# Attention heads: the division by the softmax sum done in the transposing product, and the rotary columns of two heads in one block

## What is computed

```python
def apply_rope2d(x, ang):
    xr = x.reshape(*x.shape[:-1], 2, 2, ROPE_FREQS)      # ROPE_FREQS = 16
    x1, x2 = xr[..., 0, :], xr[..., 1, :]
    out = jnp.stack([x1 * cos - x2 * sin, x2 * cos + x1 * sin], axis=-2)
    return out.reshape(x.shape)
...
q = (rms(q_a, g_qa) @ w_qb).reshape(b, n, N_HEADS, D_NOPE + D_ROPE)   # 16 x (128 + 64)
s = (q_nope @ k_nope + apply_rope2d(q_rope) @ k_rope) * scale
p = softmax(s)          # latents over 768 keys, context over its own 128
o = p @ v
```

## Time and profile before

| | |
|---|---|
| timed runs, median (lowest to highest) | 3592.96 us (3592.6 to 3592.97) |
| profiled execution | 3597.43 us |
| its span, first to last instruction | 3595.5 us |
| mean granted TensorE clock | 0.957 of full |
| TensorE busy / its weight loads | 3330.1 us (93%) / 2603.1 us (72%) |
| VectorE, ScalarE, GpSimd busy | 2101.0 (58%), 1392.9 (39%), 315.6 us (9%) |
| instructions | 40124 |

### The profile page before, as it was taken

How to read it: one execution, slowest core, us unless ns; L and a number is a source line. 1 busy time by engine, 2 the same in 40 slices (tenths; PEclk the granted TensorE clock), 3 DMA queues, 4 the chain that set the end, 5 groups by cost and what they waited for, 6 DMA issues and landing times. The chain is left out here.

```text
span 3595.5 us, 40124 instructions
## 1 busy us (share of the span) xinstructions
PE 3330.1 (93%) x16242; PEld 2603.1 (72%) x16242; DVE 2101.0 (58%) x1746; ACT 1392.9 (39%) x1234; POOL 315.6 (9%) x383
## 2 busy tenths in 40 slices
PE   6889999999997999987999999657999999999994
PEld 4678878888886999976888888554666666666662
DVE  3346555555453766653233232256888888888884
ACT  3121212221121444432121221125777777777773
POOL 0020010100000000000011210000111111111100
PEclk8999999999998999998999999858999999999997
DMA  9465554465552111106253443329999999999995
GB/s 373 176 171 203 178 185 173 164 240 191 189 176 95 38 38 38 40 19 252 102 182 134 157 169 111 121 97 368 363 398 394 381 396 395 379 398 393 382 400 201
DMA packets 140637, 796.34 MB, mean 221 GB/s; under 512 B 18416, under 2 KB 29552, under 8 KB 57360
## 3 DMA queue, kind: packets, MB, share of 16 engines
q1 hardware_dynamic: 104560, 694.46, 50.2%
q0 software_dynamic: 35952, 100.07, 9.3%
HBM read 726.60 MB, written 67.86 MB: 221 GB/s over the span
## 5 line engine op out<-in xcount | busy, mean ns | idle before, releaser
L104 PE MATMUL i_ps<-w_hi,hT_hi 128*128 128x512 f32 (+1 forms) x1440 | 568.8, 395 | 25.2 <-DVE hT_lo L559 12.9
L105 PE MATMUL i_ps<-w_lo,hT_hi 128*128 128x512 f32 (+1 forms) x1440 | 559.7, 389 | 0.0
L106 PE MATMUL i_ps<-w_hi,hT_lo 128*128 128x512 f32 (+1 forms) x1440 | 559.4, 388 | 0.0
L99 DVE TENSOR_TENSOR w_lo<-w_stage,w_hi 128x2048 fp32r<-128x2048 f32 x192 | 439.3, 2289 | 90.7 <-ACT w_hi L94 90.5
L99 DVE TENSOR_TENSOR w_lo<-w_stage_more,w_hi 128x2048 fp32r<-128x2048 f32 x192 | 439.3, 2289 | 52.2 <-ACT w_hi L94 50.3
L94 ACT ACTIVATE w_hi<-w_stage 128x2048 fp32r<-128x2048 f32 x192 | 368.3, 1919 | 163.9 <-PE e_ps L106 163.9
L94 ACT ACTIVATE w_hi<-w_stage_more 128x2048 fp32r<-128x2048 f32 x192 | 369.4, 1924 | 149.3 <-PE e_ps L106 149.3
L104 PE MATMUL e_ps<-w_hi,xgT_hi 128*80 128x512 f32 x1024 | 403.9, 394 | 6.3 <-DVE w_lo L99 5.0
L105 PE MATMUL e_ps<-w_lo,xgT_hi 128*80 128x512 f32 x1024 | 403.8, 394 | 0.0
L106 PE MATMUL e_ps<-w_hi,xgT_lo 128*80 128x512 f32 x1024 | 401.3, 392 | 0.0
L104 PE MATMUL p_ps<-w_hi,xT_hi 128*128 128x512 f32 x960 | 376.5, 392 | 18.2 <-DVE xT_lo L1437 18.2
(11 more groups left out here) (271 smaller groups left out, 4793.9 us busy)
## 6 DMA issues: line engine op xcount, KB each, us to landing
w_stage<-in_w_e SPq DMA_DIRECT2D x192, 1024.0 KB, 8.3
w_stage_more<-in_w_e SPq DMA_DIRECT2D x192, 1024.0 KB, 8.7
w_stage<-in_w_ada SPq DMA_DIRECT2D x96, 1024.0 KB, 6.0
w_raw<-in_w_in SPq DMA_DIRECT2D x64, 1024.0 KB, 4.9
w_stage<-in_w_o_gm SPq DMA_DIRECT2D x16, 1024.0 KB, 7.6
w_stage<-in_w_o_mla SPq DMA_DIRECT2D x16, 1024.0 KB, 5.7
w_stage<-in_w_out SPq DMA_DIRECT2D x16, 1024.0 KB, 5.0
acts<-evacuated POOLq DMA_DIRECT2D x60, 256.0 KB, 4.1
```

The costliest lines, as they stand in the source:

```text
L99: dve.tensor_tensor(dst, src, hi.bitcast(F32), ALU.subtract).then_inc(st.split, 1)
L104: pe.matmul(out, x_hi, w_hi, start=first, stop=False)
L105: pe.matmul(out, x_hi, w_lo, start=False, stop=False)
L106: return pe.matmul(out, x_lo, w_hi, start=False, stop=last)
```

## The change

In the heads, `divide` no longer scales the tile of probabilities: it scales the identity by the reciprocals into a diagonal matrix `diag`, and `turn` is an ordinary float32 matmul of the unscaled tile with that diagonal in place of a transpose through the identity.

The 64 rotary columns of two heads (each as its first and its second halves, instead of interleaved by 16) share one block of 128 rows, without swapped copies. Its product (`proj_rope(j)`) is done in two parts, one of each 320 tokens, in head `j - 2`. `rotate(j)` turns one such part for both heads; the swapped operand is read from the neighbouring 32 partitions. The weights of an even head have the block (1536 columns), those of an odd one don't (1024). `evac_qr` stands behind the work on the turned tile 1 on ScalarE and VectorE. The cosine and sine table is laid out anew (`table` is 128 x 2 x 640 instead of 128 x 640), and so are the rope columns of the key, of the cached keys and of `w_in`; for this the key's context rows are stored in two parts, so that `ctx_out` counts to 48. Left out below are buffers, layouts made on the host, and waits already named.

```diff
             pool.wait_ge(rot, 2)
-            pool.dma_start(O["new_krope"][0, 0], kr[:, 0, 0:D_ROPE]).then_inc(ctx_out, 16)
+            for h in range(2):
+                pool.dma_start(O["new_krope"][0, 0].rearrange("p (a h f) -> h p a f", a=2, h=2)[h],
+                               kr[:, 0, bass.ts(h, D_ROPE // 2)].rearrange("p (a f) -> p a f", a=2)).then_inc(ctx_out, 16)
...
                         if t == 0:
-                            act.wait_ge(ctx_out, 32)
+                            act.wait_ge(ctx_out, 48)
...
                 dve.tensor_tensor(kr_cos[:], raw, table[:, :, 0:D_ROPE], ALU.mult).then_inc(rot_part, 1)
-                for t in range(TT):
-                    for h in range(2):
-                        one_t = lambda ap: ap[:, t, :].rearrange("p (a h f) -> p a h f", a=2, h=2)
-                        dve.tensor_tensor(one_t(kr_sin)[:, :, h, :], one_t(raw)[:, :, 1 - h, :], one_t(table[:, :, D_ROPE:])[:, :, h, :],
-                                          ALU.mult).then_inc(rot_part, 1)
-                dve.wait_ge(rot_part, 1 + 2 * TT)
+                H = D_ROPE // 2
+                for h in range(2):
+                    dve.tensor_tensor(kr_sin[:, :, bass.ts(h, H)], raw[:, :, bass.ts(1 - h, H)], table[:, :, bass.ts(2 + h, H)],
+                                      ALU.mult).then_inc(rot_part, 1)
+                dve.wait_ge(rot_part, 3)
...
                     sp.wait_ge(pv, n - 1)
-                sp.dma_start(raw[:, n % 2, :], W_H[n]).then_inc(raw_in[n % 2], 16)
+                sp.dma_start(raw[:, n % 2, 0:split_width(n) + HW_V], I["w_heads_b" if n % 2 else "w_heads_a"][n // 2]).then_inc(raw_in[n % 2], 16)
...
             load_head(0)
-            sp.dma_start(table[:], I["rope_cols"]).then_inc(tab_in, 16)
+            sp.dma_start(table[:].rearrange("p a n -> p (a n)"), I["rope_cols"]).then_inc(tab_in, 16)
...
                     act.wait_ge(pk, n - 1)
-                act.activation(part_hi[:, b, :], raw[:, b, 0:HW_Q + HW_K], ACT.Copy).then_inc(w_hi, 1)
+                    act.wait_ge(pr, n)
+                act.activation(part_hi[:, b, 0:split_width(n)], raw[:, b, 0:split_width(n)], ACT.Copy).then_inc(w_hi, 1)
...
             def evac_qr(n):
-                act.wait_ge(rot_sum, n + 1)
-                act.activation(qr[n % 2][0:D_ROPE, :], rot[0][:], ACT.Copy).then_inc(e_hi, 1)
+                act.wait_ge(rot_sum, 2 * (n // 2) + 2)
+                act.activation(qr[n % 2][own(n), :], rot[n // 2 % 2][own(n), :], ACT.Copy).then_inc(e_hi, 1)
...
                 exp(a, 1)
+                turn_hi(a, 1)
...
                     evac_qr(a + 1)
-                turn_hi(a, 1)
...
                 dve.wait_ge(w_hi, n + 1)
-                lo(part_lo[:, b, :], raw[:, b, 0:HW_Q + HW_K], part_hi[:, b, :]).then_inc(w_lo, 1)
+                w = slice(0, split_width(n))
+                lo(part_lo[:, b, w], raw[:, b, w], part_hi[:, b, w]).then_inc(w_lo, 1)
...
-            def rotate(n):
-                dve.wait_ge(pr, n + 1)
-                if n:
-                    dve.wait_ge(e_lo, 4 * n - 2)
-                for c, (x, y) in enumerate(((0, D_ROPE), (D_ROPE, P))):
-                    dve.tensor_tensor(rot[c][:].rearrange("p (c n) -> p c n", c=2), pair[1][x:y, :, 0:N_TOK // 2],
-                                      table[x:y, :].rearrange("p (c n) -> p c n", c=2), ALU.mult).then_inc(rot_part, 1)
-                dve.wait_ge(rot_part, 2 * n + 2)
-                dve.tensor_tensor(rot[0][:], rot[0][:], rot[1][:], ALU.add).then_inc(rot_sum, 1)
+            def rotate(j):
+                dve.wait_ge(pr, j + 1)
+                if j:
+                    dve.wait_ge(rot_sum, j)
+                H = D_ROPE // 2
+                toks = bass.ts(j % 2, N_TOK // 2)
+                dst = rot[j // 2 % 2]
+                dve.tensor_tensor(dst[:, toks], pair[1][:, j % 2, 0:N_TOK // 2], table[:, 0, toks], ALU.mult).then_inc(rot_part, 1)
+                for c in range(4):
+                    dve.tensor_tensor(rot_sin[bass.ts(c, H), :], pair[1][bass.ts(c ^ 1, H), j % 2, 0:N_TOK // 2],
+                                      table[bass.ts(c ^ 1, H), 1, toks], ALU.mult).then_inc(rot_part, 1)
+                dve.wait_ge(rot_part, 5 * j + 5)
+                dve.tensor_tensor(dst[:, toks], dst[:, toks], rot_sin[:], ALU.add).then_inc(rot_sum, 1)
...
                 dve.wait_ge(e_hi, 4 * n + 2)
-                lo(qr[n % 2][D_ROPE:P, :], rot[0][:], qr[n % 2][0:D_ROPE, :]).then_inc(e_lo, 1)
+                lo(qr[n % 2][own(n + 1), :], rot[n // 2 % 2][own(n), :], qr[n % 2][own(n), :]).then_inc(e_lo, 1)
...
                 if u == 0:
-                    dve.tensor_scalar(prob_c[:], prob_c[:], red[:, 3, 1:2], None, ALU.mult)
-                dve.tensor_scalar(prob[u % 2][:], prob[u % 2][:], red[:, 3, cols(u)], None, ALU.mult).then_inc(p_ok, 1)
+                    dve.tensor_scalar(diag[2][:], M.ident[:], red[:, 3, 1:2], None, ALU.mult)
+                dve.tensor_scalar(diag[u % 2][:], M.ident[:], red[:, 3, cols(u)], None, ALU.mult).then_inc(p_ok, 1)
...
             rotate(0)
+            rotate(1)
...
                 divide(a, 1)
-                if ahead:
-                    rotate(a + 1)
+                if a + 2 < HEADS:
+                    rotate(a + 2)
                 top(a, 2)
+                turn_lo(a, 1)
...
                     evac_qr(a + 1)
-                turn_lo(a, 1)
...
         def _(pe):
-            def proj_q(n, which):
+            def proj_q(n):
                 b = n % 2
-                if which == 0:
-                    pe.wait_ge(w_lo, n + 1)
-                    if n:
-                        pe.wait_ge(e_lo, 4 * n - 1)
-                elif n:
-                    pe.wait_ge(e_lo, 4 * n)
-                    if n >= 2:
-                        pe.wait_ge(o_ev, n - 1)
-                c0 = P * which
+                pe.wait_ge(w_lo, n + 1)
+                if n:
+                    pe.wait_ge(e_lo, 4 * n - 1)
                 for half in range(2):
-                    for k in range(KG):
-                        c = slice(half * N_TOK // 2, (half + 1) * N_TOK // 2)
-                        ins = product(pe, pair[which][:, half, 0:N_TOK // 2], q_part(part_hi, b)[:, k, c0:c0 + P],
-                                      q_part(part_lo, b)[:, k, c0:c0 + P], M.qaT_hi[:, k, c], M.qaT_lo[:, k, c],
-                                      k == 0, k == KG - 1)
-                ins.then_inc(pr if which else pq, 1)
+                    ins = q_half(pair[0], half, q_part(part_hi, b), q_part(part_lo, b))
+                ins.then_inc(pq, 1)
+            def proj_rope(j):
+                if j >= 2:
+                    pe.wait_ge(w_lo, 2 * (j // 2) + 1)
+                    pe.wait_ge(e_lo, 4 * (j - 1))
+                    if j >= 3:
+                        pe.wait_ge(o_ev, j - 2)
+                q_half(pair[1], j % 2, rope_part(part_hi), rope_part(part_lo)).then_inc(pr, 1)
+            def q_half(out, half, hi, lo):
+                c = bass.ts(half, N_TOK // 2)
+                for k in range(KG):
+                    ins = product(pe, out[:, half, 0:N_TOK // 2], hi[:, k, :], lo[:, k, :], M.qaT_hi[:, k, c], M.qaT_lo[:, k, c],
+                                  k == 0, k == KG - 1)
+                return ins
...
                 b = n % 2
-                pe.wait_ge(rot_sum, n + 1)
+                pe.wait_ge(rot_sum, min(n + 2, HEADS))
+                if n >= 2:
+                    pe.wait_ge(o_ev, n - 1)
...
                         ins = pe.matmul(pair[1][:, t // 4, bass.ts(t % 4, P)], ckvT[:, k, bass.ts(t, P)],
-                                        raw[:, b, HW_Q + HW_K + k * P:HW_Q + HW_K + (k + 1) * P], start=(k == 0), stop=(k == 1))
+                                        raw[:, b, split_width(n) + k * P:split_width(n) + (k + 1) * P], start=(k == 0), stop=(k == 1))
...
                 if u == 0:
-                    pe.transpose(ctx_scores(), prob_c[:], M.ident[:])
+                    pe.matmul(ctx_scores(), prob_c[:], diag[2][:], start=True, stop=True)
                 for k in range(LAT_KEYS // P):
-                    ins = pe.transpose(pair[2 + u % 2][:, k // 3, bass.ts(k % 3, P)], prob[u % 2][:, bass.ts(k, P)], M.ident[:])
+                    ins = pe.matmul(pair[2 + u % 2][:, k // 3, bass.ts(k % 3, P)], prob[u % 2][:, bass.ts(k, P)], diag[u % 2][:], start=True, stop=True)
...
-            proj_q(0, 0)
-            proj_q(0, 1)
+            proj_q(0)
+            proj_rope(0)
+            proj_rope(1)
...
                 if ahead:
-                    proj_q(a + 1, 0)
+                    proj_q(a + 1)
...
                 turn(a, 0)
-                if ahead:
-                    proj_q(a + 1, 1)
+                if a + 2 < HEADS:
+                    proj_rope(a + 2)
```

More of the change, by code:

```diff
@@ L376, in _ @@
                 pool.wait_ge(kv_out[b], 16 * (11 - 3 * b))
-            pool.wait_ge(ctx_out, 32)
+            pool.wait_ge(ctx_out, 48)
```

(40 more changed lines are left out.)

12 lines of the change are left out of this document (6 added, 6 removed).

## The result

| | before | after |
|---|---|---|
| median of 6 runs each, us | 3592.49 (3589.69 to 3592.97) | 3605.06 (3603.17 to 3607.73) |
| profiled execution, its own time / span, us | 3597.4 / 3595.5 | 3606.19 / 3604.2 |
| heads phase: its first load to the next phase's first load, us | 487.24 | 503.82 |

The changed kernel is slower: ratio 1.0037, 95% interval 1.0024 to 1.005, which is +13.3 us (8.6 to 18). The forecast was +20, 3613 us. In a later set of runs the ratio was 1.0039 (1.0026 to 1.0053).

The account below looks back on a forecast made before the run. TensorE's own queue was taken to bound the steady heads. Fifteen intervals of +0.91 us gave 13.6; 13.6 + 2.6 (start) + 2.6 (end) + 1.5 (clock) = +20 us on 3592.96, so 3613 us, range 3602 to 3628.

Parts of the forecast that it names:

- head 14 to 15: Interval without proj_rope behind turn(14, 0): a 2.5 us pause replaces 3.60 us of work, about the same sum, +0.91 us.
- Part 1: Turns in the heads: products with a diagonal replace 400 transposes, adding 2.98 us of TensorE a head, 48 us over 16.
- rival A: Turns: a product with the diagonal is one record like a transpose, 0.109 us; -23 us, 3570 us, faster; 6%.
- rival C: Turns: a product costs four transposes, 0.39 us; +89 us, 3682 us; 2%.
- Part 2: Rotary query products: 12 a head in place of 24, taking away 1.76 us a head, 28 us over all.
- Part 3: Before scores(a, 2): shorter proj_rope no longer covers pT_lo of tile 0, a new pause of 0.66 us a head.
- Rival B: Before scores(a, 2): no new pause, no clock dips, rotations of 2.4 us; 3600 us, at the edge of no measurable change; 7%.
- Part 4: Before scores(a, 3): the old pause of 0.97 us a head goes, 0.1 us in hand, rotate reckoned at 3.05 us.
- rival D: Rotations take 4 us, so a 0.85 us pause returns before scores(a, 3); +15 us, 3628 us; 15%.
- The ends and the clock: Heads phase: +2.6 us at its start, +2.6 at its end, +1.5 for half clock behind two new 2.5 us pauses.
- What costs nothing: First phase: kr_sin in two instructions and a second small store cost nothing; 0.6 us once if the store's cover were gone.
- keep the full clock to the end: End of the heads: if products count as clock activity, 22.7 us of work takes 5 us less; left out of the sum.

Follow-up runs that it names:

- experiments 2: The kernel before with only the transposes replaced by products with the scaled diagonal: ratio 1.0091, a steady head of 30.53 us.
- the order alone: The kernel before with only evac_qr moved behind the work on turned tile 1 on ScalarE and VectorE: ratio 0.9949, a steady head of 27.385 us.
- experiment 5: The changed kernel with 12 plain query products of the next head moved ahead of proj_rope, evac_qn and mix reordered: ratios 1.0014 and, run again, 1.0012.
- experiment 3: The changed kernel with the transposes and the division of prob put back, rotary blocks and new order kept: ratio 0.9952, a steady head of 27.23 us.

## Why the prediction was right, and where its sizes were off

The forecast of slower held, and 3605.06 lies in its range, near the lower end. Each step against the heads phase of the first profile:

| | forecast, us | measured, us |
|---|---|---|
| to the first turn (rotations, clock) | 2.6 and part of 1.5 | 35.45 - 30.97 = 4.5 |
| 14 steady heads | 14 x 0.91 = 12.7 | 14 x 0.809 = 11.3 |
| head 14 to 15 | 0.9 | 27.86 - 28.67 = -0.8 |
| end | 2.6 | 32.23 - 30.65 = 1.6 |
| sum | 20.3 | 16.6 |

- **Part 1, the turns.** Right in kind: two records a product, slots of 0.105 to 0.111 us. Mis-sized by a little: the turns of a head take 5.38 us where 5.46 was reckoned, and the transposes they replace took 2.51, not 2.48, so 2.87 us a head were added instead of 2.98. The first 768-record row refutes rival A (one record), and the slot refutes rival C: products and transposes are 0.21 and 0.097 us apart, 2.2 and not 4. The Trainium skill's "TensorE: Matmul & The Clock Gate" (Terms) states four times; the trace does not agree. Its advice in "Perfetto Trace Analysis" (Transposes), to use a transpose where a transpose is meant, held: experiments 2 and 3 put the price of not doing so at 30 to 33 us.
- **Part 2, the rotary products.** 192 records gone from the 768, as forecast. No run has the rotary block without the new order, so its -1.76 us a head shows only inside sums: from the order alone to the changed kernel it is +2.87 - 1.76 + 0.67 = 1.78, measured 29.163 - 27.385 = 1.78.
- **Part 3, the new pause.** 0.66 forecast, 0.67 measured, and experiment 5 took it away. Rival B is out.
- **Part 4, the old pause.** Gone, as forecast; `rotate` took 3.1 us where 3.05 was reckoned, so rival D is out. The 0.1 us in hand was 0.25. What the prediction did not say is that this rests on the diagonal, by its longer turns and its shorter division (the 0.33 us that I had called worth nothing): without it 0.84 us come back (experiment 3). The two parts of the change are not additive: alone they give +2.18 and 27.229 - 28.354 = -1.13 a head, together 0.81 and not 1.05.
- **Head 14 to 15.** This is the term that was furthest off, by 1.7 us. The work in it was reckoned right: behind `turn(14, 0)` TensorE waits 2.50 us, as forecast. But I added only new dips to the base. In the profile before this interval took 28.67 us, 1.6 of them for a dip that my own rows showed, and I did not ask whether it would stay. The changed kernel's first profile had none there (27.86 us), the second had one (29.45 us). Dip against dip the interval moved by +0.8, close to the 0.9; against the first profile it moved by -0.8, and that is the luck of one execution.
- **The ends and the clock.** The rotations cost +2.7 us at the start (2.6 forecast), and the clock 1.7 more in one profile and nothing in the other. The end grew by 1.6 and 0.8 us instead of 2.6. With the diagonal alone it grew by 2.61. That this is the forecast number is in part chance, for the clock differs too: over the whole end it is 0.78 before and 0.75 with the diagonal alone. In the two profiles of the changed kernel it is 0.80 and 0.83, and the second has the shorter end. The first 26 us of the end had 0.81 in the changed kernel's first profile and 0.74 before, as this row of busy time shows, of before, from its head 15's first turn:

```profile
1595.50:1621.50 26.00, 17.18 (x67) 14.25 (x65) 9.48 (x17) 6.05 (x11) 0.00 (x0) 0.74 0.03 13
```

  In experiment 3 the end took 29.33 us, 1.3 less than before, and the rotary part did not shorten it: every wait in it is as long as before within 0.15 us, and the granted clock is nearly the same on the mean (0.77, before 0.78). But less of the half clock fell on work and more on waits: the ten products behind the first wait took 1.67 us, where before they took 2.72. Nor did the products keep the full clock to the end, the case which the prediction named and left out of its sum.
- **What costs nothing.** The first phase held: 1.0003. But the criterion "wrong if the time outside the phase moves by more than 2 us" was a bad one: it moved by 7.9 us in the profile (3108.3 to 3100.4), and by nearly as much where nothing outside the heads was changed (3101.5 with the diagonal alone, and with the order alone).

What is left between +16.6 us in the phase (+15.8 in the second profile) and +13.3 and +14 in the timed runs is within the interval of 8.6 to 18. I don't claim a cause for it.

## What to carry to other kernels

Where TensorE is the bound, as here, a float32 product of 128 x 128 in the place of a transpose cost 2.2 times its time, and the 21 us of work saved on VectorE, which had time to spare, did not pay for it. When work is taken out from between two instructions that depend on one another, ask what that work covered: here 1.76 us of products taken away left a pause of 0.67, and moving other work into the gap gave it back. Before reckoning with a new order of work, try the cheapest piece of it alone: two moved lines were worth 18 us, as much as the whole rotary part that contains them.

## What the runs showed of the hardware

- VectorE takes as long for 32 partitions as for 128: 487 ns for 32x320 (64 times) and 0.49 us for 128x320 in the same `rotate`. Four parts with different first partitions came 0.52 us apart, each behind the end of the one before. The Trainium skill's "VectorE: DVE Perf Modes" (Two Vector instructions with no wait between them) has such instructions held where their first quadrants differ; the trace agrees.
- A pause of TensorE does not always bring the half clock. Behind the wait for `rot`, 3.29 us idle, `proj_v(0)` ran at 0.67; behind the same wait with 3.51 us idle in the second profile it ran its 28 records in 3.15 us (1161.71 to 1164.86), at full clock. One such dip costs 1.6 to 1.7 us, and it moved from place to place between executions of one program.
- In the order alone, with transposes as before, no dip came ahead of head 15 (a granted clock of 1.00 over the interval, where before had 0.94), and with products one came in one execution and not in the other. So in these runs the clock does not follow from the turns being transposes or products.
